# Two transformer blocks on one core: input tiles first in the queue, and ScalarE's copies spread over the steps of the first attention

## The chip, the cores and the metric

The kernel runs on one core of a Trainium2 chip. The metric is the device time of one execution in microseconds, and the time of a kernel is the median of its runs. Engines are named as usual: TensorE (PE) multiplies, VectorE (DVE) and ScalarE (ACT) do elementwise work, GpSimd (POOL) and SyncE (SP) here mostly issue transfers.

## The reference

One input `x` of 1 x 1024 x 1024 floats passes through two blocks. Only the beginning of the first one matters here:

```python
h = rms_norm(x, g_pre_mix)                 # mean of squares over the 1024 features
z = h @ w_in                               # 1024 x 2560
q, k, v, zu, zv = split(z)                 # 8 heads of 64
attn = dilated_attention(q, k, v, rel_bias)  # three windows (128,1), (512,4), (2048,16)
sgu = spatial_gating(gelu(zu), gelu(zv), ...)
mix = concat([attn, sgu]) @ w_out
x = x + rms_norm(mix, g_post_mix)
x = x + rms_norm(square(relu(rms_norm(x) @ w_ff1)) @ w_ff2, g_post_ffn)
```

The second block (modulated norms, a sparse attention that picks 256 keys by an index score, a convolution, another feed-forward layer) follows and isn't touched.

## The kernel before

Activations are held transposed, feature by token: `XT` is 128 partitions x 8 tiles x 1024 tokens. A weight matrix comes as slabs of 128 x 1024 (512 KB). Each product of a slab is made from three fp32r products: high part of the weights times high part of the input, high times low, low times high. ScalarE makes a slab's high part `whi` (L768), VectorE its low part `wlo` (L1715); an input tile is split in the same way into `XH` (L792) and `XL` (L1762). The order on every engine is written out by hand and tied together by semaphores.

**The prologue.** SP issues the transfers in this order: slab 0, `vec` (all vectors), `cst` (the constants: identity, ones, and others), the eight tiles of `XT`, slab 1. `vec` and `cst` count on `params_loaded`, the eight tiles on one semaphore, `x_loaded`. POOL loads `HOT` (a one-hot table) and `RB` (relative biases). TensorE waits for the constants and both tables, then multiplies `RB` by `HOT` (L1295, six products of 512 columns) into three PSUM tiles. VectorE copies them to `TAB` with the sign changed (L1792), from where POOL stores them to DRAM for later loads. VectorE next makes the low parts of slabs 0 and 1, and then adds up the squares of the tiles (L1722, L1725), which ScalarE makes (L778) into two buffers `SQ` after it has made the two high parts and all tiles are there. TensorE sums the total over partitions (L1257), VectorE and ScalarE turn this into the reciprocal root and a diagonal `DG` (L1749 to L1752, root on ScalarE L786), TensorE spreads it over all partitions (L1280). Then each tile is scaled (`HF`, L1770) and split, and the first two slabs are multiplied as the split tiles come (`product_pair`, L1237). Between its root and its splits ScalarE makes small copies that are needed much later (L805, L807) and a Silu (L809). After the splits ScalarE makes slab 2's high part, and evicts slab 0's product through a Gelu (L831); TensorE then turns it (L1312).

**The first attention.** It runs over 8 heads x 8 steps, `n = 8 h + d`. At each step TensorE makes scores by key (L1413), the values weighted by the probabilities of step `n - 3` (L1433, L1438, accumulated in `TP[1]` over a head's eight steps), and a guard product for step `n + 12` (L1386, of which VectorE takes the minimum, L1885). VectorE subtracts the bias strip (L1899), ScalarE takes Exp (L913). Between these, ScalarE has work per head:

```python
if d == 4 and h + 1 < HEADS:
    guard_row(h + 1)          # L881, the row of guard values, before that step's Exp
...                           # Exp of step n
if n in (10, 26):
    round_pair(n // 16 + 2)   # L861, L862: KR and QR of the next pair of heads
if d == 1 and 1 <= h < HEADS - 1:
    operands(h + 1)           # L872, L873: KA and QA of the next head
if d == 2 and h:
    sums_copy(h - 1)          # L890: TP[1] to OL; the next head's values wait for it
if d == 3 and h:
    inverse(h - 1)            # L896, L899: Ln and Exp of the sums
```

POOL scales a finished head, loads its bias strips and copies the row into `QA`.

Of the kernel before, what the change touches and what calls it, by code (L numbers as in the profile page):

```python
# [25 lines left out]
D = 1024  # L26
KT_N = D // P
# [3 lines left out]
HEADS = 8  # L31
# [16 lines left out]
RMS_EPS = 1e-6  # L48
# [94 lines left out]
def build(nc, slabs, ada, xT, vecs, lnrow, sgu_wT, rel_bias, positions, consts, hot, outT, dbg=None):  # L143
# [5 lines left out]
    def sem(name):  # L149
        return ctx.enter_context(nc.semaphore(name))  # L150
# [160 lines left out]
    hi_ready, lo_ready = sem("hi_ready"), sem("lo_ready")  # L311
    slab_done = sem("slab_done")
    psum_free = [sem(f"psum_free{b}") for b in range(2)]
    params_loaded, x_loaded, sgu_loaded = sem("params_loaded"), sem("x_loaded"), sem("sgu_loaded")
    hot_loaded, tab_made, tab_stored = sem("hot_loaded"), sem("tab_made"), sem("tab_stored")
    tab_copied = sem("tab_copied")
    bias_loaded = [sem(f"bias_loaded{b}") for b in range(2)]
# [175 lines left out]
    @block.sync  # L493
    def _(sp):
        def load(g, b):
            sp.dma_start(raw[b][:, :], slabs[bass.ds(g, 1), :, :].rearrange("a p n -> p (a n)")
                         if not isinstance(g, int) else slabs[g, :, :]).then_inc(raw_loaded[b], 16)

        load(0, 0)
        sp.dma_start(vec[:, :], vecs).then_inc(params_loaded, 16)  # L500
        sp.dma_start(cst[:, :], consts).then_inc(params_loaded, 16)
        for k in range(KT_N):
            sp.dma_start(XT[:, k, :], xT_v[:, k, :]).then_inc(x_loaded, 16)
        load(1, 1)
        first_loop, last_loop = (IN2 + 16 - 2) // 2, (OUT2 + 3 - 1) // 2
        assert IN2 % 2 == 0 and OUT2 % 2 == 1

        def next_slab(g):

            sp.wait_ge(lo_ready, g - 1)  # L510
            load(g, g % 2)

        def load_pairs(first, end):

            with sp.Fori(first, end) as t:
                for j in range(2):
                    sp.wait_ge(lo_ready, t * 2 + (1 + j))
                    load(t * 2 + (2 + j), j)

        def to_phases(j):  # L520

            sp.wait_ge(glu_ready, j + 1)
            sp.wait_ge(pool_seq, 3)
            sp.wait_ge(roped, 10)
            if j > 1:
                sp.wait_ge(conv_out, OUT_OF_TILE * (j - 1))
            for q in range(PHASES):
                for g in range(PHASES):
                    sp.dma_start(XP[j % 2][CB * q:CB * (q + 1), g, :], CUQ[CB * g:CB * (g + 1), j, q, :]).then_inc(phases_ready, 16)

        def to_channels(j, g):

            sp.wait_ge(conv_evicted, PHASES * j + g + 1)
            if j == 0:
                sp.wait_ge(conv_used, PHASES)
                sp.wait_ge(wt_moved, 1)
            for at_p in range(PHASES):
                p = PHASES - 1 - at_p
                sp.dma_start(YC[CB * g:CB * (g + 1), j, p * S // PHASES:(p + 1) * S // PHASES],
                             XP[j % 2][CB * at_p:CB * (at_p + 1), g, 0:S // PHASES]).then_inc(conv_out, 16)  # L540

        load_pairs(0, first_loop)
        next_slab(IN2 + 16)
        to_phases(0)
        next_slab(IN2 + 17)
        next_slab(IN2 + 18)
        to_phases(1)
        next_slab(OUT2)
        next_slab(OUT2 + 1)
        for j in range(PE_TILES):  # L550
            for g in range(PHASES):
                to_channels(j, g)
            if j + 2 < PE_TILES:
                to_phases(j + 2)
        next_slab(OUT2 + 2)
        load_pairs(last_loop, (STREAM - 2) // 2)
        sp.wait_ge(out_stored, 16 * KT_N)
# [199 lines left out]
    def _(act):  # L757
# [35 lines left out]
                               bias=bias(k) if bias else 0.0).then_inc(x_hi, 1)  # L793


        act.wait_ge(params_loaded, 32)
        hi(0, 0, 0)
        hi(1, 1, 0)
        squares(XT, lambda k: (x_loaded, 16 * KT_N))
        norm_root()  # L800
        act.wait_ge(params_loaded, 32)

        for q in range(PHASES):
# [3 lines left out]
                act.activation(phase_b[of_q, 4 * g:4 * g + 4], vec[CB * g:CB * (g + 1), VCOL["conv_b"]:VCOL["conv_b"] + 4],  # L807
                               ACT.Copy).then_inc(eye_ready, 1)
        act.activation(silc[:, :], vec[:, VCOL["c"]:VCOL["c"] + 8], ACT.Silu).then_inc(silc_ready, 1)  # L809
        splits(KT_N, 0)  # L810

        def to_qk(dst, scale, off):
            def body(m, g, b, h):
# [48 lines left out]
            act.activation(QR[m % 2][:, :].rearrange("p (t c) -> p t c", c=P)[:, :, ::-1],  # L862
                           QT[:, m, :].rearrange("p (t c) -> p t c", c=P), ACT.Copy, scale=-1.0).then_inc(rounded, 1)

        def operands(h):

            own = halves(h)[0]
            if h < 2:
                act.wait_ge(turned, 16)
            else:  # L870
                act.wait_ge(st_ready, NT * (h - 1))
            act.activation(KA[h % 2][0:DH, ::-1], KT[own, h // 2, :], ACT.Copy).then_inc(operands_ready, 1)  # L872
            act.activation(QA[h % 2][0:DH, :].rearrange("p (c u) -> p c u", c=4), by_class(QT[own, h // 2, :]),  # L873
                           ACT.Copy).then_inc(operands_ready, 1)

# [25 lines left out]
        def dilated_attention():  # L901

            act.preload_act_table_set("natural_log_exp_and_others")
            operands(0)
            guard_row(0)
            operands(1)
            round_pair(1)
            for n in range(NT * HEADS):
                h, d = divmod(n, NT)
                if d == 4 and h + 1 < HEADS:  # L910
                    guard_row(h + 1)
                act.wait_ge(st_taken, n + 1)
                act.activation(PT[n % 4][:, :], PT[n % 4][:, :], ACT.Exp).then_inc(pt_ready, 1)  # L913
                if n in (10, 26):
                    round_pair(n // 16 + 2)
                if n == 40:
                    hi_next(OUT1, OUT1 % 2, OUT1 // 2)
                if d == 1 and 1 <= h < HEADS - 1:
                    operands(h + 1)
                if d == 2 and h:  # L920
                    sums_copy(h - 1)
                if d == 3 and h:
                    inverse(h - 1)
                if n in (52, 60):
                    attended(n // 8 - 6)
            sums_copy(HEADS - 1)
            inverse(HEADS - 1)
# [123 lines left out]
        n = 0  # L1051
# [152 lines left out]
    def _(pe):  # L1204
# [84 lines left out]
            fill(ahead, g)  # L1289


        pe.wait_ge(params_loaded, 32)
        pe.wait_ge(hot_loaded, 32)
        for c in range(N_TABLE // HALF):
            last = pe.matmul((G[0], G[1], TP[0])[c // 2][0:HEADS, c % 2, :], RB[0:33, :], HOT[0:33, c * HALF:(c + 1) * HALF],  # L1295
                             start=True, stop=True)
        last.then_inc(tab_made, 1)
        pe.wait_ge(tab_copied, 1)
        norm_stat(KT_N, SSQ)
        norm_spread(DG)  # L1300


# [392 lines left out]
    def _(dve):  # L1695
# [37 lines left out]
            seq(dve.tensor_scalar(aa[:, :], aa[:, :], -0.5, 1.5, ALU.mult, ALU.add))  # L1733
            seq(dve.tensor_tensor(rstd[:, :], y0[:, :], aa[:, :], ALU.mult))

        def norm(width, eps, tiles=KT_N, sq=SQ, ssq=SSQ, dg=DG, first=0, stat=TP[1], between=None, last_on_pe=False, summed=None):
            for k in range(first, tiles - 1 if last_on_pe else tiles):
                add_square(k, sq, ssq)
            if between:
# [7 lines left out]
            else:  # L1747
# [3 lines left out]
            reciprocal_root()  # L1751
            t_diag.inc(dve.tensor_tensor(dg[:, :, :], ident.unsqueeze(1).broadcast_to([P, NT, P]),  # L1752
                                         rstd[:, :].unsqueeze(2).broadcast_to([P, NT, P]), ALU.mult))
            t_spread.wait(dve, 1)

        def split_norm(scale, bias, base):
# [30 lines left out]
                behind(KT_N - 1)  # L1787


        dve.wait_ge(tab_made, 1)  # L1790
        for b, made in enumerate((Gf[0], Gf[1], TPf[0])):
            last = dve.tensor_scalar(TAB[0:HEADS, b * S:(b + 1) * S], made[0:HEADS, :], -1.0, None, ALU.mult)  # L1792
        last.then_inc(tab_copied, 1)
        lo(0, 0)
        lo(1, 1)
        norm(D, RMS_EPS)
        dve.wait_ge(tab_stored, 16)
        split_norm(lambda k: V("g_pre_mix", k), None, 0)

# [613 lines left out]
```

## Time and profile before

| | |
|---|---|
| median of 3 runs | 2792.48 us (2790.01 to 2794.37) |
| profiled execution, its time | 2793.15 us |
| its span | 2791.4 us |
| busy: TensorE, VectorE, ScalarE, GpSimd | 2641.2, 1351.2, 836.0, 251.5 us |
| chain that ended last, by engine | PE 81%, DVE 9%, ACT 5%, issue 4% |
| mean granted TensorE clock | 0.978 |

The busy time of TensorE holds its waits inside a pipelined stream, so 95% of the span is no measure of how near it is to its peak. The chain says what the end of the kernel hung on, step by step back to the start; work on other engines that isn't in the chain costs nothing.

### The profile page before, as it was taken

The page shows a single profiled execution, that of the slowest core. Times are in us where ns is not written, and L with a number is a line of the kernel's source. Part 1 is how long each engine was busy: PE and PEld are TensorE (multiplying, and loading weights), DVE is VectorE, ACT ScalarE, POOL GpSimd, SP SyncE. Part 2 cuts the span into 40 slices and gives each one's busy share as a digit, 9 for nine tenths or more (in the row PEclk, how much of TensorE's full clock was granted, in tenths as well). Part 3 has the DMA queues.
Part 4 walks back from the last instruction along what each step waited for, and adds up shares of the span by engine and source line. Part 5 has one row for each costly group of instructions (what it writes and reads, how often), then busy time and mean ns, then how long its engine had stood idle before and what let it go on. Part 6 is the DMA issues. An engine that isn't in the chain of part 4 may idle for free.

```text
span 2791.4 us, 28672 instructions
## 1 busy us (share of the span) xinstructions
PE 2641.2 (95%) x11363; PEld 2088.6 (75%) x11363; DVE 1351.2 (48%) x1585; ACT 836.0 (30%) x1083; POOL 251.5 (9%) x269
## 2 busy tenths in 40 slices
PE   5999999989999999999999988898999999999996
PEld 3887667867888888888765766665878888888884
DVE  5242666356334343345748878786453232232333
ACT  3211345333112021121325575435332021120221
POOL 0000222002111121121001000211000000000000
PEclk9999999999999999999899998999999999999997
DMA  3211110214222222231310111001111111111111
GB/s 111 89 46 50 42 55 32 68 60 151 91 80 87 76 90 83 76 105 61 136 41 5 46 39 39 4 8 50 67 38 53 46 46 53 45 53 45 46 53 68
DMA packets 50376, 169.68 MB, mean 61 GB/s; under 512 B 7544, under 2 KB 11128, under 8 KB 50232
## 3 DMA queue, kind: packets, MB, share of 16 engines
q1 hardware_dynamic: 32544, 104.27, 11.4%
q0 software_dynamic: 17728, 63.98, 6.7%
q8 instruction: 72, 1.18, 0.2%
q14 instruction: 32, 0.25, 0.0%
HBM read 152.05 MB, written 12.68 MB: 59 GB/s over the span
## 4 chain that ended last, share of the span: by engine, by line
PE 81%; DVE 9%; ACT 5%; issue 4%; DMA 0%; SPq 0%; DVEq 0%; POOL 0%; ACTq 0%; POOLq 0%
PE G L1219 61%; PE G L1237 4%; PE G L1413 2%; PE TP L1642 2%; ACT TK L1071 2%; PE G L1560 1%; PE TP L1433 1%; PE TP L1386 1%; PE TP L1257 1%; DVE JUNK L2245 1%; PE G L1576 1%; ACT T L1057 1%; PE TP L1280 1%; PE TP L1438 1%; DVE wlo L1715 1%
## 5 line engine op out<-in xcount | busy, mean ns | idle before, releaser
L1219 PE MATMUL G<-XH,whi 128*128 128x512 f32 x1712 | 539.2, 396 | 15.2 <-DVE wlo L1715 13.1
L1219 PE MATMUL G<-XL,whi 128*128 128x512 f32 x1712 | 529.9, 391 | 0.0
L1219 PE MATMUL G<-XH,wlo 128*128 128x512 f32 x1712 | 529.8, 391 | 0.0
L768 ACT ACTIVATE whi<-raw 128x1024 fp32r<-128x1024 f32 x184 | 193.8, 1053 | 732.6 <-PE G L1219 671.0
L1219 PEld LDWEIGHTS G<-XH,whi 128*128 128x128 f32 x1712 | 319.8, 189 | 86.5 <-DVE wlo L1715 15.2
L1219 PEld LDWEIGHTS G<-XL,whi 128*128 128x128 f32 x1712 | 322.7, 189 | 67.8
L1219 PEld LDWEIGHTS G<-XH,wlo 128*128 128x128 f32 x1712 | 322.7, 188 | 67.8
L1219 PE MATMUL G<-UH,whi 128*128 128x512 f32 x1024 | 316.9, 391 | 0.0
L1219 PE MATMUL G<-UL,whi 128*128 128x512 f32 x1024 | 315.6, 389 | 0.0
L1219 PE MATMUL G<-UH,wlo 128*128 128x512 f32 x1024 | 315.5, 389 | 0.0
L1715 DVE TENSOR_TENSOR wlo<-raw,whi 128x1024 fp32r<-128x1024 f32 x184 | 224.3, 1220 | 149.4 <-ACT whi L768 149.1
L1219 PEld LDWEIGHTS G<-UH,wlo 128*128 128x128 f32 x1024 | 192.3, 188 | 40.0
L1219 PEld LDWEIGHTS G<-UL,whi 128*128 128x128 f32 x1024 | 192.3, 188 | 40.0
L1219 PEld LDWEIGHTS G<-UH,whi 128*128 128x128 f32 x1024 | 191.1, 188 | 38.6
L2026 DVE SCALAR_TENSOR_TENSOR XT<-G,mod,XT 128x1024 f32<-128x1024 f32 x32 | 41.1, 1285 | 249.1 <-PE G L1219 249.1
L2012 DVE TENSOR_TENSOR USQ<-RELU 128x1024 f32<-128x1024 f32 x32 | 39.2, 1225 | 192.2 <-ACT RELU L999 192.1
L995 ACT ACTIVATE RELU<-RELU 128x1024 f32<-128x1024 f32 x32 | 34.0, 1062 | 243.1 <-DVE RELU L2006 224.0
L1071 ACT ACTIVATE TK<-SC,cand 128x512 f32<-128x512 f32 (+2 forms) x93 | 82.8, 892 | 67.2 <-DVE cand L2132 67.2
L2026 DVE SCALAR_TENSOR_TENSOR XT<-G,XT 128x1024 f32<-128x1024 f32 x24 | 29.4, 1225 | 151.3 <-PE G L1219 151.3
L1991 DVE TENSOR_REDUCE RED<-ADA 128x128 f32<-128x1024 f32 x48 | 95.0, 1979 | 0.0
L999 ACT ACTIVATE RELU<-G 128x1024 f32<-128x1024 f32 x32 | 32.9, 1028 | 205.0 <-PE G L1219 205.0
L1885 DVE CUSTOM_DVE_ANT_0 JUNK<-TP,BIAS 128x1024 bf16<-128x1024 f32 x54 | 66.2, 1226 | 50.5 <-PE TP L1386 50.5
(304 smaller groups left out, 3195.2 us busy)
## 6 DMA issues: line engine op xcount, KB each, us to landing
raw<-slabs SPq DMA_DIRECT2D x184, 512.0 KB, 3.4
ADA<-ada POOLq DMA_DIRECT2D x48, 512.0 KB, 3.8
x_spill<-XT POOLq DMA_DIRECT2D x2, 4096.0 KB, 12.9
BIAS<-tab_spill POOLq DMA_DIRECT2D x8, 960.0 KB, 4.9
XT<-xT SPq DMA_DIRECT2D x8, 512.0 KB, 10.0
XRE<-xT POOLq DMA_DIRECT2D x8, 512.0 KB, 3.9
XRE<-x_spill POOLq DMA_DIRECT2D x8, 512.0 KB, 3.7
XT<-x_spill POOLq DMA_DIRECT2D x1, 4096.0 KB, 13.8
```

The lines of the kernel that those rows point to most:

```text
L768: act.activation(whi[b][:, :, :].rearrange("p k n -> p (k n)"), raw[b][:, :], ACT.Copy).then_inc(hi_ready, 1)
L995: act.activation(RELU[:, :], RELU[:, :], ACT.Square).then_inc(usq_ready, 1)
L1071: t_counted.inc(act.activation((TK1, TK2)[t_counted.n % 2][:, 0:w], SC[:, score_at(TOPK_TILE + n):score_at(TOPK_TILE + n + 1)], ACT.Sign, ...
L1219: last = pe.matmul(G[b][:, half, :], w[b][:, k, :], x[:, k, half * HALF:(half + 1) * HALF], start=(at_k == 0 and n == 0), stop=(at_k == KT ...
L1237: last = pe.matmul(G[b][:, half, :], w[b][:, k, :], x[:, k, half * HALF:(half + 1) * HALF], start=(at_k == 0 and n == 0), stop=(at_k == KT ...
L1413: last = pe.matmul(G[n % 4 // 2][:, n % 2, j * 2 * P:(j + 1) * 2 * P], keys, queries, start=True, stop=True)
L1642: pe.matmul(TP[1][:, u % 2, :], VO2[r][:, c, :], PT2[n % 4][:, :], start=(c == 0), stop=(c == i)).then_inc(p2_used, 1)
L1715: dve.tensor_tensor(wlo[b][:, :, :].rearrange("p k n -> p (k n)"), raw[b][:, :], whi[b][:, :, :].bitcast(F32).rearrange("p k n -> p (k n)" ...
L1885: dve.tensor_tensor_reduce(out=JUNK1[:, :], in0=flat(guard_out(p)), in1=BIAS[h % 2][:, 896 - i * P:896 - i * P + S], scale=1.0, scalar=HIG ...
L1991: dve.tensor_reduce(RED[a % 2][:, :], ADA[a % 2][:, :, :].rearrange("p k n -> p n k"), AX.X, ALU.add).then_inc(ada_red, 1)
L2012: dve.tensor_tensor(USQ[:, :], RELU[:, :], RELU[:, :], ALU.mult).then_inc(usq_ready, 1)
L2026: ins = dve.scalar_tensor_tensor(out=XT[:, m - 8, :], in0=Gf[b], scalar=scale(m - 8), in1=XT[:, m - 8, :], op0=ALU.mult, op1=ALU.add)
```

## The change

In the prologue SP issues the eight tiles of `XT` first, each with a semaphore of its own, then the constants, slab 0, the vectors and slab 1. ScalarE squares each tile when it has landed, before the high parts of slabs 0 and 1, and makes its small copies and the Silu after the splits. VectorE adds the squares first, then copies the table, waits for constants and vectors, and makes the low parts of slabs 0 and 1 after the diagonal (the new argument `ahead` of `norm`). TensorE starts the table products without a wait for the constants, waits for constants and vectors after them, and sums the squares before it waits for the table copies.

In the first attention `operands` becomes `key_operand` (after step 0) and `query_operand` (after step 3); `inverse` moves from step 3 to step 4, and the rounding of the next pair from `n` = 10, 26 to 14, 30.

```diff
@@ SP
+        for k in range(KT_N):
+            sp.dma_start(XT[:, k, :], xT_v[:, k, :]).then_inc(tile_loaded[k], 16)
+        sp.dma_start(cst[:, :], consts).then_inc(params_loaded, 16)
         load(0, 0)
         sp.dma_start(vec[:, :], vecs).then_inc(params_loaded, 16)
-        sp.dma_start(cst[:, :], consts).then_inc(params_loaded, 16)
-        for k in range(KT_N):
-            sp.dma_start(XT[:, k, :], xT_v[:, k, :]).then_inc(x_loaded, 16)
         load(1, 1)
@@ ScalarE, prologue
-        act.wait_ge(params_loaded, 32)
+        squares(XT, lambda k: (tile_loaded[k], 16))
         hi(0, 0, 0)
         hi(1, 1, 0)
-        squares(XT, lambda k: (x_loaded, 16 * KT_N))
         norm_root()
+        splits(KT_N, 0)
         act.wait_ge(params_loaded, 32)
...
         act.activation(silc[:, :], vec[:, VCOL["c"]:VCOL["c"] + 8], ACT.Silu).then_inc(silc_ready, 1)
-        splits(KT_N, 0)
@@ ScalarE, first attention
-        def operands(h):
+        def key_operand(h):
...
             act.activation(KA[h % 2][0:DH, ::-1], KT[own, h // 2, :], ACT.Copy).then_inc(operands_ready, 1)
+
+        def query_operand(h):
+
+            own = halves(h)[0]
             act.activation(QA[h % 2][0:DH, :].rearrange("p (c u) -> p c u", c=4), by_class(QT[own, h // 2, :]),
                            ACT.Copy).then_inc(operands_ready, 1)
...
-                if n in (10, 26):
-                    round_pair(n // 16 + 2)
                 if n == 40:
                     hi_next(OUT1, OUT1 % 2, OUT1 // 2)
-                if d == 1 and 1 <= h < HEADS - 1:
-                    operands(h + 1)
+                if d == 0 and 1 <= h < HEADS - 1:
+                    key_operand(h + 1)
                 if d == 2 and h:
                     sums_copy(h - 1)
-                if d == 3 and h:
+                if d == 3 and 1 <= h < HEADS - 1:
+                    query_operand(h + 1)
+                if d == 4 and h:
                     inverse(h - 1)
+                if n in (14, 30):
+                    round_pair(n // 16 + 2)
@@ TensorE
-        pe.wait_ge(params_loaded, 32)
         pe.wait_ge(hot_loaded, 32)
...
         last.then_inc(tab_made, 1)
+        pe.wait_ge(params_loaded, 32)
+        norm_stat(KT_N, SSQ)
         pe.wait_ge(tab_copied, 1)
-        norm_stat(KT_N, SSQ)
         norm_spread(DG)
@@ VectorE
+            if ahead:
+                ahead()
             t_spread.wait(dve, 1)
...
+        for k in range(KT_N):
+            add_square(k)
         dve.wait_ge(tab_made, 1)
...
         last.then_inc(tab_copied, 1)
-        lo(0, 0)
-        lo(1, 1)
-        norm(D, RMS_EPS)
+        dve.wait_ge(params_loaded, 32)
+        norm(D, RMS_EPS, first=KT_N, ahead=lambda: (lo(0, 0), lo(1, 1)))
```

## Rows read from the trace of the kernel before

**Rows 1.** The chain of waits, 0 to 110 us: start, length in us, what.
```profile
1.78 8.12 DMA cst<-consts
...
20.39 3.47 DVE TAB L1792 x3
23.86 2.27 DVE wlo L1715 x2
...
36.19 3.56 PE TP L1257 x16
...
50.21 24.23 PE G L1237 x96
```

**Rows 2.** Timeline, 0 to 50 us: start, length, engine, line, what [idle before].
```profile
4.83 1.28 ACT L768 ACT_TABLE_LOAD   x1 [4.83 <-DMA raw<-slabs]
...
21.24 1.06 ACT L768 ACTIVATE whi<-raw 128x1024 fp32r<-128x1024 f32 x1 [10.26 <-DMA raw<-slabs]
...
26.84 9.20 DVE L1725 TENSOR_TENSOR SSQ<-SSQ,SQ 128x1024 f32<-128x1024 f32 x7
...
40.09 0.21 ACT L805 ACTIVATE eye<-cst 32x32 f32<-32x32 f32 x1
...
42.62 3.78 PE L1280 MATMUL TP<-DG,cst 128*128 128x512 f32 x4 [2.88 <-DVE DG L1752]
...
45.87 0.21 ACT L809 ACTIVATE silc<-vec 128x8 f32<-128x8 f32 x1
```

**Rows 3.** The source view of L503, the input tiles: durations, first and last issue.
```profile
L503 SPq DMA_DIRECT2D XT<-xT x8: 432/538/1035, 2.3 to 6.9; - x8
...
DMA to landing us min/median/max: 7.5/10.0/13.1
```

**Rows 4.** DMA issues, 0 to 60 us: KB each, us to landing.
```profile
tab_spill<-TAB POOLq DMA_DIRECT2D x1, 96.0 KB, 3.4
RB<-rel_bias POOLq DMA_DIRECT2D x1, 1.0 KB, 7.6
```

**Rows 5.** Timeline, 60 to 80 us, ScalarE and TensorE.
```profile
70.45 1.06 ACT L768 ACTIVATE whi<-raw 128x1024 fp32r<-128x1024 f32 x1 [5.73 <-PE G L1237]
71.53 1.28 ACT L831 ACT_TABLE_LOAD   x1
72.82 1.03 ACT L831 ACTIVATE TT<-G 128x1024 f32<-128x1024 f32 x1
...
74.28 1.03 PE L1312 MATMUL TP<-cst,TT 128*128 128x128 f32 x8
```

**Rows 6.** Windows, heads 1 and 2: length, busy PE, PEld, DVE, ACT, POOL, PEclk, DMA.
```profile
331.06:358.53 27.47, 24.90 (x103) 17.54 (x102) 16.47 (x24) 12.97 (x19) 3.28 (x6) 0.88 0.16 51
358.53:382.24 23.71, 22.69 (x104) 16.68 (x104) 16.49 (x24) 11.19 (x16) 6.75 (x8) 1.00 0.17 59
```

**Rows 7.** Timeline of the first attention, heads 1, 2 and 7.
```profile
352.46 2.05 PE L1433 MATMUL TP<-PT,VONE 128*128 128x256 f32 x4 [2.57 <-ACT OL L890]
...
375.07 1.08 DVE L1899 TENSOR_TENSOR PT<-G,STRIP 128x512 f32<-128x512 f32 x1
375.18 2.01 ACT L873 ACTIVATE QA<-QT 64x1024 f32<-64x1024 f32 x1
...
377.75 1.06 ACT L890 ACTIVATE OL<-TP 128x512 f32<-128x512 f32 x2
...
378.48 1.10 PE L1433 MATMUL TP<-PT,VONE 128*128 128x256 f32 x4 [0.93 <-ACT OL L890]
378.77 0.63 ACT L913 ACTIVATE PT<-PT 128x512 f32<-128x512 f32 x1
...
381.99 0.27 ACT L881 ACTIVATE ROW<-TP 8x128 f32<-8x128 f32 x1 [0.55 <-PE TP L1393]
...
493.50 1.10 PE L1433 MATMUL TP<-PT,VONE 128*128 128x256 f32 x4 [0.66 <-ACT OL L890]
```

**Rows 8.** The source view of L1433, 320 to 505 us: idle before it, times.
```profile
ACT OL L890: 9.3, 7
```

More of the change, by code:

```diff
@@ L313, in build @@
     psum_free = [sem(f"psum_free{b}") for b in range(2)]
-    params_loaded, x_loaded, sgu_loaded = sem("params_loaded"), sem("x_loaded"), sem("sgu_loaded")
+    params_loaded, sgu_loaded = sem("params_loaded"), sem("sgu_loaded")
+    tile_loaded = [sem(f"tile_loaded{k}") for k in range(KT_N)]
     hot_loaded, tab_made, tab_stored = sem("hot_loaded"), sem("tab_made"), sem("tab_stored")
@@ L903, in dilated_attention @@
             act.preload_act_table_set("natural_log_exp_and_others")
-            operands(0)
+            key_operand(0)
+            query_operand(0)
             guard_row(0)
-            operands(1)
+            key_operand(1)
+            query_operand(1)
             round_pair(1)
@@ L1734, in reciprocal_root, with norm @@
             seq(dve.tensor_tensor(rstd[:, :], y0[:, :], aa[:, :], ALU.mult))
-        def norm(width, eps, tiles=KT_N, sq=SQ, ssq=SSQ, dg=DG, first=0, stat=TP[1], between=None, last_on_pe=False, summed=None):
+        def norm(width, eps, tiles=KT_N, sq=SQ, ssq=SSQ, dg=DG, first=0, stat=TP[1], between=None, last_on_pe=False, summed=None, ahead=None):
             for k in range(first, tiles - 1 if last_on_pe else tiles):
```

## Prediction

> **What bounds the kernel.** I read the chain that ended last first, because the table of shares alone (TensorE busy 95% of the span) would say that only matmuls count. The chain agrees for the long middle of the kernel, but its first 50 us run through other engines [rows 1]: a load, table matmuls, table copies and low parts on VectorE, the sum of squares, a column sum, and then the first product at 50.21. Whatever is taken out of that prologue is taken out of the time, since nothing later waits for a clock of its own: slabs are loaded when low parts are done. Next I read the timeline and the windows of the first attention, where TensorE is the longest engine but has short holes. The reader should look there for who ends each hole. The source view of L1433 names ScalarE's copy L890 for 9.3 us in 7 holes [rows 8].
>
> **Prologue, before.** The matmuls on the table start at 9.9, when the constants land (1.78 + 8.12), and end at 20.4. VectorE then copies the table (3.47), makes two low parts (2.27) and only then adds squares, to 36.1 [rows 1]. The squares run late too: ScalarE waits for slab 1 until 21.24 [rows 2], behind the wait for all input tiles. The column sum takes 3.56 and the first product starts 14.0 after the sum's start (50.21 less 36.19) [rows 1].
>
> **Prologue, after.** The column sum (L1257) needs three things:
> (a) The table matmuls, on the same queue: 20.4 if they start as before. They now need only the hot table and RB. RB is a transfer of 1 KB behind the hot table and took 7.6 [rows 4], so it must have landed shortly before the constants did; I take no change. Bounds: it lands no earlier than raw slab 0 did, 4.83 [rows 2], which would end the table matmuls 5 earlier (of which item (c) leaves 0.6 as gain); above, I allow the 1.5 us between two tiles (next item).
> (b) The squares and additions. Tile 0 landed at 2.3 + 7.5 = 9.8 and tile 7 at 6.9 + 13.1 = 20.0 [rows 3], 1.46 apart. First in the queue, tile 0 lands where raw slab 0 did, 4.83 [rows 2], and tile 7 at 4.83 + 7 x 1.46 = 15.1. The other bound: 896 KB (a slab, the vectors, the constants) no longer stand ahead of tile 7, at 1.46 per 512 KB 2.6 us; that gives 17.4. After landing, one square (ScalarE, 1.06 as for its neighbours) and one addition: the seven took 9.20, so 1.31 each [rows 2]. The additions end between 17.5 and 19.8, under the 20.4 of the table matmuls either way. I take 17.5; a tile stream as late as 21.2 would give the rival below.
> (c) The vectors, whose semaphore TensorE now waits for here. Slab 1, last in the queue, landed at 21.24 [rows 2]; the bytes are the same, so I keep that end, and the vectors land one slab earlier, about 19.8.
> So the sum starts at 20.4 instead of 36.19: **15.8 us**. The table copies (3.47) start at 20.4 as well and lie beside the sum (3.56), both end at 23.9; the variance needs both. Two low parts (2.27) lie beside the spread matmuls (3.78 [rows 2]), which are in front of the next VectorE work; without this cover they would cost 2.3. ScalarE makes the high parts of slabs 0 and 1 until about 22.3 and then loads the table for the root (1.28, as the load at 71.53 [rows 5]): 23.6, just under 24.0. SP issues the same transfers in another order, and only slab 0 lands later, by about 14, to about 18.5, while its high part is first wanted by a low part at 27. POOL's queue is not changed; its table store still follows the table copies at 23.9, 3.4 to landing [rows 4], before VectorE asks for it at 30.6.
> ScalarE's small copies (identity blocks, biases, Silu) took from 40.09 to 46.08 [rows 2] beside the spread. They move behind the eighth split. Before, ScalarE was idle for 5.73 there until slab 0's product ended [rows 5]. 5.99 do not fit in 5.73, so slab 2's high part, the table load and the Gelu eviction are 0.3 late. The eviction had ended at 73.85 and TensorE took it up at 74.28 [rows 5], 0.4 later. Cost: 0 expected, 0.3 at worst.
> Here a rule of the Trainium skill speaks against the change: page "ScalarE: Activation LUTs", section "What ACT_TABLE_LOAD costs", puts a switch of sets at about 2.66 us, since a drain comes with the load. With the trace the sum stays at 2763; with the page it would be the 2766 of the third rival. The load at 71.53 was followed by its activation 1.29 later [rows 5], so the trace doesn't show the drain.
>
> **First attention, before.** A head is 8 steps. TensorE may overwrite the accumulator of the last head only after L890 has copied it out, and L890 sits behind the exponentials of step 2 and, before those, both operand copies of step 1. In head 2 the scores of step 2 were ready for Exp at 376.15 (375.07 + 1.08), but ScalarE was in the QA copy (2.01), so L890 began at 377.75 and TensorE at 378.48, 0.93 late [rows 7]. In heads 1 and 3 the KR and QR copies come on top (about 1.06 each, as every ScalarE tile of 1024 columns [rows 2]): 2.57 late, and then the clock is down: 0.88 granted in that window, 1.00 in the next (full speed is 2.4 GHz, the other level 1.2) [rows 6, 7]. The holes of heads 1 to 6 are 9.3 less the last head's 0.66: 8.6 [rows 7, 8]. The clock costs, per event: window 27.47 against 23.71 is 3.76, less the hole's excess 1.64, 2.1; or 12% of 27.47, 3.3. I take 2.6, twice: 5.2.
>
> **After.** Step 0 has the KA copy (1.06; with Exp 1.7, in a step of 23.71 / 8 = 3.0), step 1 nothing, step 2 L890, step 3 the QA copy, step 4 the inverse (2.1), step 6 the rounding pair (2.1). Exp of step 2 then runs at 376.15, L890 at 376.7, and TensorE may go on 0.73 after that (378.48 less 377.75), at 377.4; it is itself free at 378.48 - 0.93 = 377.55. So the hole closes with 0.1 to spare. Queued behind the QA copy are the ROW copy and Exp of step 4: Exp of step 3 ran at 378.77, so QA ends by 381.3, while ROW could start at 381.99 - 0.93 = 381.06 [rows 7]; TensorE needs ROW only after a 1.1 us group of value matmuls. Behind the inverse stands Exp of step 5, used three steps later. KR and QR are first used in step 20 or 36 and now made at 14 and 30. Gain **8.6 + 5.2 = 13.8 us**; lower bound with the smaller clock term 12.8, upper 15.2.
>
> **Sum.** 15.8 + 13.8 = 29.6. The profiled execution took 2793.15 (span 2791.4), so 2763.6; it stands 0.7 above the median of 2792.48, so the median becomes **2763**.
>
> **Rivals.**
> Late squares: the eight tiles share the queues with the hot table so badly that tile 7 lands at the end of the stream, 21.2. Then 21.2 + 1.06 + 1.31 = 23.6 is the start of the column sum, 3.2 later: 2766. For it: tiles took up to 13.1 to land. Against: they are first in their queue now.
> Attention keeps its holes: 0.1 to spare is thin, and the last head, which has no operand copies, still had one of the seven holes [rows 8]. If 0.9 stays in each of six heads and only the clock loss and the excess go, 5.5 are missing: 2768. Against: that head's steps are shorter, for want of guard matmuls.
> Switch of sets: if a load in the middle of ScalarE's work costs twice its 1.28, the root's ends at 24.9, 0.9 after the variance, and the Gelu eviction, behind Silu's load and its own, is 0.3 + 2.6 late against the 0.4 to spare: 0.9 + 2.5 = 3.4 is missing, 2766. Against: the activation at 72.82 begins with the end of the load at 71.53 [rows 5]. This is how the change would go by the Trainium skill's rule of that page and section.
> Other side, slower: ScalarE's ROW copy. If it came late enough to hold TensorE 2.57 in each of heads 1 to 6, each would lose that and the clock's 2.6, 5.2 x 6 = 31, over the gain of 29.6: 2794. It decides from about 3.4 us later than worked out (0.8 of it the cover by value matmuls), where I find 0.2.
> No effect: the prologue is moved but the first product still waits for something at 50. I see no such thing: the slabs are in by 21.2 and the table is stored by 23.9 + 3.4.
>
> **How the numbers follow.** Forecast 74% (own range 2760 to 2766), late squares 8%, attention holes 8%, switch of sets 5%, opposite side 1.5%, no effect 1.5%, and 2% for a gain beyond 2760 (the spread and the first matmuls at the higher clock: half of 3.78 for the one, an estimate, and as much for the other). 0.2% of this time, 5.6 us, is about what a measurement can tell from no change. Every case but two ends far below it. Range 2759 to 2769: it takes in the three small rivals, the clock term's ends (+1.0, -1.4) and RB's landing (+1.5).
>
> **What would show it.** In the new profile: table matmuls from about 9.9 to 20.4; column sum right behind them; the first product at 34.4; no hole before the turn L1312 at about 58.5; L1433 with one hole for L890 (the last head) rather than seven; no window of the attention under 1.00; last exponential of the attention 29 to 30 earlier than at 502. Wrong if: table matmuls begin after 11.5, VectorE's additions outlast them, or heads take more than 22.8.

## The result and the profile after

The changed kernel took 2772.03 us in the median of 4 executions (2768.82, 2769.16, 2774.9, 2775.36), the kernel before 2791.48 (4 executions, 2790.01 to 2794.37). The ratio is 0.9928 (95% interval 0.9914 to 0.9942): 0.7% faster, clear of noise, but 9 us above my 2763 and 3 above the upper end of my range.

The profiled execution is the one of 2768.82 us, with a span of 2767.1, 24.3 less than before. Its chain of waits, 0 to 110 us, has these pieces (start, length, what):

```profile
2.09 7.17 DMA RB<-rel_bias
...
16.30 3.41 PE TP L1302 x4
19.71 3.52 PE TP L1265 x16
...
26.25 3.77 PE TP L1288 x4
...
38.62 19.34 PE G L1245 x84
57.96 0.87 PE TP L1320 x8
```

The column sum now follows the table matmuls without a gap, at 19.7 where it stood at 36.2 [rows 1]; additions, table copies and low parts are gone from the chain. The timeline of the same stretch shows what the steps of the prediction are about, the last square, the additions, the second high part and the load for the root, the root, the two low parts and the first product:

```profile
10.85 7.87 DVE L1733 TENSOR_TENSOR SSQ<-SSQ,SQ 128x1024 f32<-128x1024 f32 x6 [2.54 <-ACT SQ L779]
...
16.17 1.06 ACT L779 ACTIVATE SQ<-XT 128x1024 f32<-128x1024 f32 x1 [0.22 <-DMA XT<-xT]
...
19.72 1.06 ACT L769 ACTIVATE whi<-raw 128x1024 fp32r<-128x1024 f32 x1 [0.52 <-DMA raw<-slabs]
...
20.79 1.28 ACT L787 ACT_TABLE_LOAD   x1
...
23.52 0.21 ACT L787 ACTIVATE root<-var 128x8 f32<-128x8 f32 x1 [1.45 <-DVE var L1757]
...
26.02 2.35 DVE L1723 TENSOR_TENSOR wlo<-raw,whi 128x1024 fp32r<-128x1024 f32 x2
...
33.81 1.16 PE L1245 MATMUL G<-XH,whi 128*128 128x512 f32 x2 [3.81 <-DVE XL L1772]
```

The additions end at 18.7, a microsecond before the table matmuls do. The first product starts at 33.81 in place of 50.21: 16.4 less.

In the first attention the source view of the value matmuls (L1441, which was L1433) names one hole for the copy of the accumulator where there were seven [rows 8], the one of the last head; and the windows of heads 1 to 3 (columns as in [rows 6]) are even and at full clock:

```profile
  ACT OL L894: 0.7, 1
```

```profile
321.22:343.66 22.44, 22.35 (x103) 16.56 (x103) 16.45 (x25) 8.71 (x13) 3.28 (x6) 1.00 0.19 62
343.66:366.08 22.42, 22.33 (x104) 16.54 (x103) 16.47 (x25) 13.06 (x18) 6.76 (x8) 1.00 0.17 62
366.08:388.54 22.46, 22.38 (x104) 16.57 (x103) 16.44 (x25) 11.22 (x16) 6.75 (x8) 1.00 0.17 63
```

From the first scores to the first product behind the attention (L1245, L1237 before) it takes 169.84, against 184.33 before: 14.5 less. So both halves of the change did a little more than forecast, 16.4 + 14.5 = 30.9. Of these 24.3 arrived. The rest is lost between them, in the stretch from the last turns of the values (L1358, L1350 before) to the first scores. There the kernel before took 32.08 and the changed one 39.01, with the same instructions. Windows of that stretch, the changed kernel and then the kernel before:

```profile
271.68:310.69 39.01, 37.96 (x135) 25.36 (x134) 24.06 (x32) 16.59 (x15) 11.86 (x15) 0.69 0.07 26
```

```profile
288.16:320.24 32.08, 30.48 (x135) 19.95 (x134) 23.77 (x32) 16.57 (x15) 11.87 (x15) 0.89 0.09 31
```

The counts (x135, x32, x15) are equal, and so is the busy time of ScalarE and GpSimd to 0.02 us; TensorE has 7.5 us more of busy time, and its clock was granted at 0.69 in place of 0.89. No engine waits for anything new. 30.9 - 6.9 + 0.3 (the rest of the kernel, 2286.57 against 2286.83) = 24.3, the whole difference of the spans.

### The profile page after: what moved, and what is told of

Read it like the earlier page. It is cut to its first block, busy times and chain, and to the rows that moved or that the text cites. A ratio compares the mean times of both kernels' runs of the same rounds, so it can differ in the third digit from the quotient of the medians.

```text
span 2767.1 us, 28672 instructions
## 1 busy us (share of the span) xinstructions
PE 2641.7 (95%) x11363; PEld 2092.1 (76%) x11363; DVE 1351.1 (49%) x1585; ACT 836.1 (30%) x1083; POOL 251.8 (9%) x269
## 4 chain that ended last, share of the span: by engine, by line
PE 83%; DVE 8%; ACT 4%; issue 4%; DMA 0%; SPq 0%; DVEq 0%; POOL 0%; ACTq 0%; POOLq 0%
PE G L1227 62%; PE G L1245 4%; PE G L1421 2%; PE TP L1650 2%; ACT TK L1079 1%; PE G L1568 1%; PE TP L1394 1%; PE TP L1441 1%; PE TP L1446 1%; DVE JUNK L2256 1%; PE TP L1265 1%; PE G L1584 1%; ACT T L1065 1%; PE TP L1288 1%; PE G L1255 1%
## 5 line engine op out<-in xcount | busy, mean ns | idle before, releaser
L1227 PE MATMUL G<-XH,whi 128*128 128x512 f32 x1712 | 540.3, 397 | 14.3 <-DVE wlo L1723 12.4
L1245 PE MATMUL G<-XH,whi 128*128 128x512 f32 x192 | 63.2, 411 | 26.1 <-DVE XL L2326 9.3
## 6 DMA issues: line engine op xcount, KB each, us to landing
XT<-x_spill POOLq DMA_DIRECT2D x1, 4096.0 KB, 13.8
```

Source lines behind the costliest of these rows:

```text
L1227: last = pe.matmul(G[b][:, half, :], w[b][:, k, :], x[:, k, half * HALF:(half + 1) * HALF], start=(at_k == 0 and n == 0), stop=(at_k == KT ...
L1245: last = pe.matmul(G[b][:, half, :], w[b][:, k, :], x[:, k, half * HALF:(half + 1) * HALF], start=(at_k == 0 and n == 0), stop=(at_k == KT ...
```

## Experiments

Two theories. **C**: the granted clock falls in that stretch in some executions and not in others, since TensorE's work is thin there; the change has no part in it. **S**: the new order makes the stretch longer by itself. "Stretch" below is always that from the last value turns to the first scores, and a "dip" is a time in it at the lower clock, 1.2 GHz. Some expectations count the stretch from about 5.9 us later: their 33.1 and 26.2 are the 39.0 and 32.1 of this text.

### e1, e5, e10, e13: the changed kernel again

No edit. What was expected:

> The changed kernel once more, unaltered. Its profile has the work between the last value turn (L1358) and the first scores (L1421) of the first attention in 33.1 us, where the kernel before took 26.2, with the granted clock at 0.50 from 280 to 300 us. Theory C (the clock falls there or not by chance of time, the instructions being the same): over the executions the time takes more than one value, steps of some 6 us apart (2769 and 2775 so far), and in this profile the stretch may take 26 or 33. Theory S (the new order makes that stretch longer by itself): the stretch takes 33 again and every run the same time within 2 us.

> The changed kernel once more, on whatever chip this falls, beside the three below. Theory C (the time is a base plus what the clock takes in each execution): the runs lie between 2757 and 2775, ordered by their mean granted clock, some 2 us for each 0.001. Theory S: one value, 2759 or 2769.

> The changed kernel again, beside its version with full rows on one chip. So far 15 executions of it: nine between 2756.8 and 2762.2, six between 2768.7 and 2775.4. By that rate two of these lie above 2766.

> The changed kernel, fifth time: 21 executions so far, 15 of them under 2763 and six between 2768 and 2776. Theory C: again mostly 2757 to 2760, one or two higher, and a higher one has the lower granted clock.

| | executions, us | median | mean clock of each |
|---|---|---|---|
| first | 2768.8, 2769.2, 2774.9, 2775.4 | 2772.0 | 0.976, 0.976, 0.972, 0.972 |
| e1 | 2756.8, 2759.2, 2759.2, 2759.4, 2759.5, 2772.0 | 2759.3 | 0.981, 0.981, 0.981, 0.981, 0.981, 0.973 |
| e5 | 2757.2, 2757.5, 2759.7, 2762.2, 2768.7 | 2759.7 | 0.980, 0.981, 0.981, 0.980, 0.977 |
| e10 | 2757.4, 2757.4, 2757.4, 2757.7, 2759.2, 2759.5 | 2757.6 | 0.981, 0.980, 0.981, 0.981, 0.981, 0.979 |
| e13 | 2756.9, 2757.3, 2759.1, 2759.2, 2769.0, 2775.1 | 2759.2 | 0.981, 0.980, 0.981, 0.981, 0.976, 0.974 |

The time isn't one value, and the high ones are those with the lower clock. The kernel before spreads more: 66 executions between 2786.5 and 2809.0, median 2794.3. Over the 62 of them that were run beside the experiments, a straight line gives 2.2 us for each 0.001 of mean clock. Of e10's six I expected two above 2766; none was. The ratio in e1 is 0.9871 (0.9843 to 0.9900), in e13 0.9878 (0.9848 to 0.9908). The stretch took 32.1, 29.2, 29.3 and 32.1 in these four profiles. Windows of e10's:

```profile
271.25:300.55 29.30, 27.66 (x135) 18.59 (x134) 23.78 (x32) 16.57 (x15) 11.87 (x15) 1.00 0.09 34
```

Same kernel, same counts, 9.7 us less than in the first profile, at 1.00 in place of 0.69. Theory S falls. The timelines of the two show where they part. TensorE, first profile, then e10:

```profile
279.05 1.56 PE L1394 MATMUL G<-KR,QR 64*128 64x512 f32 x4 [0.61 <-DVE nega L1896]
280.54 1.97 PE L1375 MATMUL TP<-cst,NAT 128*128 128x128 f32 x8
282.44 2.07 PE L1394 MATMUL G<-KR,QR 64*128 64x512 f32 x4
```

```profile
278.63 1.16 PE L1394 MATMUL G<-KR,QR 64*128 64x512 f32 x4 [0.60 <-DVE nega L1896]
279.72 1.10 PE L1375 MATMUL TP<-cst,NAT 128*128 128x128 f32 x8
280.75 1.19 PE L1394 MATMUL G<-KR,QR 64*128 64x512 f32 x4
```

The hole before the guard products is the same to 0.01 us, and so is the work that led up to it (16 turns in 2.01, the guards in 2.1); within the next four products the one clock fell to 1.2 GHz and stayed there until about 303, the other stayed at 2.4.

There is a second place. In e1 the clock held behind that hole and fell behind the next one, 10 us later:

```profile
289.11 1.19 PE L1394 MATMUL G<-KR,QR 64*128 64x512 f32 x4 [0.57 <-DVE nega L1896]
290.25 1.72 PE L1260 MATMUL TP<-XH 128*128 128x512 f32 x4
```

So the 32.1 of e1, of e13 and of the kernel before is a dip too, a short one: without any the stretch takes 29.2 or 29.3.

### e2 and e3: one half of the change each

e2 is the changed kernel with the attention order of before:

```diff
+                if n in (10, 26):
+                    round_pair(n // 16 + 2)
                 if n == 40:
                     hi_next(OUT1, OUT1 % 2, OUT1 // 2)
-                if d == 0 and 1 <= h < HEADS - 1:
+                if d == 1 and 1 <= h < HEADS - 1:
                     key_operand(h + 1)
+                    query_operand(h + 1)
                 if d == 2 and h:
                     sums_copy(h - 1)
-                if d == 3 and 1 <= h < HEADS - 1:
-                    query_operand(h + 1)
-                if d == 4 and h:
+                if d == 3 and h:
                     inverse(h - 1)
-                if n in (14, 30):
-                    round_pair(n // 16 + 2)
```

e3 is the kernel before with the reverse of this edit.

> The prologue of the changed kernel with the attention order of before. Prologue by itself: 16.4 us by the first product's start (50.2 to 33.8). If the stretch before the attention runs at half clock here too (theory C in its form 'where it falls in time decides', the stretch being at the same time as in the changed kernel; and theory S in the form that the prologue's order does it): 16.4 - 6.9 = 9.5 less than before, about 2782, and its window 280 to 300 shows 0.50. If the attention's new order were the cause: 2775 and a window at 1.00.

> The attention order of the changed kernel with the prologue of before. By the chain the attention from first scores to last values took 184.4 before and 169.9 after, 14.5 less. Theory C: the stretch before the attention stands at the same time as in the kernel before, so it keeps its 26 us and the gain is 14.5: 2777. If the new order costs the 6.9 in that stretch (theory S, since its first copies are on ScalarE there): 2784 and a half-speed window at 296 to 316 us.

e2: median 2777.1 (12 executions, 2771.4 to 2792.5), ratio 0.9932 (0.9911 to 0.9953). e3: 2776.2 (12 executions, 2772.8 to 2791.1), ratio 0.9941 (0.9919 to 0.9962). Their medians come to 21.5 and 22.4 below the 2798.6 of the kernel before beside them. The two gains add up to more than the 39.3 between the medians of the kernel before and e1 on that chip; each median holds what the clock took in its own executions. In e2's profile the first product is at 33.6, as in the changed kernel, and the stretch took 29.3. In e3's, where the prologue is that of before, it took 38.9 at 0.69:

```profile
286.64:325.57 38.93, 37.89 (x134) 25.36 (x133) 24.02 (x32) 16.58 (x15) 11.86 (x15) 0.69 0.08 26
```

So the dip comes with the old prologue too, some 15 us later in time, and it stays away in e2's profiled execution, whose prologue is the new one: neither the prologue's order nor the place in time makes it by itself. My form of theory C that had it depend on the place in time alone was wrong for both runs.

e2 shows something else. Its attention has the seven holes of before, and took 187.4 in place of 184.3. One of them and the windows around it:

```profile
362.23 1.10 PE L1440 MATMUL TP<-PT,VONE 128*128 128x256 f32 x4 [0.94 <-ACT OL L894]
```

```profile
311.50:339.10 27.60, 25.03 (x104) 17.59 (x103) 16.70 (x25) 12.99 (x18) 3.28 (x6) 0.88 0.14 51
339.10:362.90 23.80, 22.86 (x93) 17.05 (x94) 14.78 (x22) 8.93 (x13) 6.75 (x8) 0.85 0.16 59
```

The clock was down in the first and in the second window, where the kernel before had 1.00 in its second [rows 6]: the hole of 2.6 cost the clock for longer in this execution. e3 and every profile of the changed kernel have 169.8 to 169.9 for the attention.

### e7: the operand copies back at step 1

The changed kernel with both operand copies at step 1; the rounding pair stays at steps 14 and 30, and the inverse at step 4:

```diff
-                if d == 0 and 1 <= h < HEADS - 1:
+                if d == 1 and 1 <= h < HEADS - 1:
                     key_operand(h + 1)
+                    query_operand(h + 1)
                 if d == 2 and h:
                     sums_copy(h - 1)
-                if d == 3 and 1 <= h < HEADS - 1:
-                    query_operand(h + 1)
```

> The changed kernel, but both operand copies at step 1 and so in front of the copy L890 of step 2, as before; the rounding pair stays at steps 14 and 30. If the operand copies make the holes of 0.9 in each of heads 1 to 6 (0.9 x 6 = 5.5) and the rounding pair made the rest: six holes of 0.7 to 1.0 for L890 in the profile, none of 2.6, no clock loss in the heads, 5.5 more than the changed kernel: about 2765. If holes of that size too cost the clock: windows under 1.00 within the heads and 2770 or more. If the holes are gone even so: 2759.

Median 2765.8 (6 executions, 2763.7 to 2779.1), beside 2759.7 for the changed kernel (e5, same chip). The attention took 175.5, 5.7 more than 169.8. The holes in heads 1 to 3:

```profile
340.62 1.10 PE L1440 MATMUL TP<-PT,VONE 128*128 128x256 f32 x4 [0.68 <-ACT OL L894]
...
364.13 1.10 PE L1440 MATMUL TP<-PT,VONE 128*128 128x256 f32 x4 [0.96 <-ACT OL L894]
...
387.38 1.10 PE L1440 MATMUL TP<-PT,VONE 128*128 128x256 f32 x4 [0.68 <-ACT OL L894]
```

Holes of 0.7 to 1.0, none of 2.6, and no loss of clock (1.00 over the whole attention), as expected. The six holes come to 4.9 (5.6 in seven, less the last head's 0.7), and the copies in front of L894 cost 5.7 in all. The other 8.8 of the 14.5 came with the moves that e7 keeps, rounding pair and inverse together; the inverse was not tried alone. The profiled execution itself had the dip in the stretch (39.0) and took 2775.7.

### e12: the old order of transfers

```diff
-        for k in range(KT_N):
-            sp.dma_start(XT[:, k, :], xT_v[:, k, :]).then_inc(tile_loaded[k], 16)
-        sp.dma_start(cst[:, :], consts).then_inc(params_loaded, 16)
         load(0, 0)
         sp.dma_start(vec[:, :], vecs).then_inc(params_loaded, 16)
+        sp.dma_start(cst[:, :], consts).then_inc(params_loaded, 16)
+        for k in range(KT_N):
+            sp.dma_start(XT[:, k, :], xT_v[:, k, :]).then_inc(tile_loaded[k], 16)
         load(1, 1)
```

> The changed kernel, but SP issues slab 0, vectors, constants, tiles, slab 1 as before; all else as changed. Prologue by its steps: tile 7 then lands at about 20, its square ends at 21.1, the additions at 22.4, and the column sum starts there in place of 19.4: 3.0 later, first product at 36.5 in place of 33.5, time 3 above the changed kernel's, 2762. If the tile order were the whole prologue gain: first product near 50. If it gave nothing: 33.5.

Timeline of its profile, the last square and the column sum:

```profile
18.75 1.06 ACT L779 ACTIVATE SQ<-XT 128x1024 f32<-128x1024 f32 x1 [0.27 <-DMA XT<-xT]
...
21.47 3.54 PE L1265 MATMUL TP<-cst,SSQ 128*128 128x1 f32 x16 [2.40 <-DVE SSQ L1733]
```

The column sum waits 2.40 for the additions and starts at 21.5, in e10 on the same chip at 19.2; the first products are at 35.6 and 33.3. So of the prologue's 16.4 the order of the transfers is worth 2.3 (I expected 3.0) and the order of the work on VectorE, ScalarE and TensorE the rest, 14.1, by subtraction. Median 2764.7 (2759.8 to 2778.5) beside 2757.6; its stretch took 44.6 in the profile, the longest of all: the dip that began behind the hole of 0.60 lasted until the first scores.

### e4, e6, e11, e14, e9: all rows in the first of each guard pair

The first eight guard products are made twice, for TensorE's sake alone. Here the first of each pair reads all 128 rows of the same tiles; its result is overwritten.

```diff
-            for _ in range(2 if p < NT else 1):
+            for rows in ((slice(0, P), own) if p < NT else (own,)):
                 for half in range(2):
-                    last = pe.matmul(guard_out(p)[:, half, :], QR[h // 2 % 2][own, i * P:(i + 1) * P],
-                                     KR[h // 2 % 2][own, half * HALF:(half + 1) * HALF], start=True, stop=True)
+                    last = pe.matmul(guard_out(p)[:, half, :], QR[h // 2 % 2][rows, i * P:(i + 1) * P],
+                                     KR[h // 2 % 2][rows, half * HALF:(half + 1) * HALF], start=True, stop=True)
```

> The changed kernel; only the first of the two identical guard products of each of the first eight guards reads all 128 rows of the same tiles in place of 64 (its result is overwritten by the second, so output and number of columns are unchanged). Theory C with the addition that thin work in TensorE (64 rows, transposes, short holes) lets the clock fall in that stretch: with all rows it stays up more often, 26 us in place of 33, and the time is 6 to 7 lower than the changed kernel's: 2762. Theory S, or a clock that looks at holes alone: no change, 2769 to 2775.

> The changed kernel with the first of each pair of guard products on 128 rows, again (the pair before it on one chip: 2759.7 against 2759.3 by the median, but its profile had no window under 1.00 between 40 and 560 us, and the stretch before the first scores took 29.5 in place of 32.1). If full rows keep the clock up in that stretch: again no such window in the profile, 29.5 us, and no run above 2762; if it was chance: a dip there in the profile, or runs above 2766 as often as the changed kernel has them.

> The changed kernel with full rows in the first product of each guard pair again. So far 11 executions, all between 2757.1 and 2760.7. If full rows prevent the dip: again none above 2762, stretch 29.5 in the profile. If it was the chip and chance: as many above 2766 as the changed kernel has beside it.

> Full rows in the first product of each early guard pair, fourth time: 17 executions so far between 2755.1 and 2760.7. If full rows prevent the dip, none above 2762 again, and the stretch from the last value turns to the first scores at 29.5 or 29.6 as in all four of its profiles. One above 2766 refutes it.

22 executions between 2755.1 and 2760.7, median 2759.7, mean 2759.1; the changed kernel's 27 have the median 2759.2 and the mean 2762.4, and eight of them lie between 2768.7 and 2775.4. The stretch took 29.54, 29.58, 29.61 and 29.55. By the median nothing is gained, where e4's text expected 6 to 7: in three of the four profiles the part behind the attention took 2286.9 to 2288.3, in e1's and e13's 2284.1 and 2284.3. Windows of e4's:

```profile
271.85:301.39 29.54, 28.37 (x134) 17.74 (x133) 23.75 (x32) 16.57 (x15) 11.88 (x15) 1.00 0.09 34
```

If the eight had fallen on the 49 executions by chance, none of them would lie among these 22 in 1 of 200 cases. Without the first four, which had no such kernel run beside them, it is 4 of 23 against 0 of 22, 1 in 17: likely, not settled.

The edit changes more than the rows. The hole before the third guard, where the long dips begin, was 0.60 or 0.61 wherever each guard was made twice on 64 rows; with full rows the first four products last longer (2.70 in place of 2.1 us) and the hole is 0.20, in all five profiles. e4's:

```profile
276.31 2.70 PE L1394 MATMUL G<-KR,QR 128*128 128x512 f32 x8
279.21 1.36 PE L1394 MATMUL G<-KR,QR 128*128 128x512 f32 x4 [0.20 <-DVE nega L1896]
```

So rows and hole were changed together, and no run here tells which of them keeps the clock. For the rows speaks that the next hole hardly changed (0.54 for 0.57) and the short dips behind it are gone as well: none in five profiles, where four of the seven 64-row profiles that came past the first hole without a dip have one. That is too few to settle it.

e9 is the same edit in the kernel before.

> The kernel before, with only the first of each of its eight pairs of guard products on all 128 rows. If full rows keep the clock up before the first scores: that stretch takes 29.5 in place of 32.1 or 39 in the profile, and no such dip; the rest of the runs keeps its spread (the holes of 2.6 in heads 1 and 3 still cost the clock), so 2786 to 2802 and a median some 3 to 7 under the kernel before. If it was chance: the same spread and median as before.

12 executions between 2788.7 and 2795.4, median 2790.8, against 2786.5 to 2807.0, median 2793.8; ratio 0.9990 (0.9975 to 1.0005). None of the twelve is above 2796, where six of the 17 beside them are, but the medians can't be told apart. The stretch took 29.6 at 1.00:

```profile
287.92:317.53 29.61, 28.43 (x135) 17.77 (x133) 23.80 (x32) 16.57 (x15) 11.88 (x15) 1.00 0.10 34
```

### e8: each early guard once

```diff
-            for _ in range(2 if p < NT else 1):
+            for _ in range(1):
```

> The changed kernel without the repeated product in each of the first eight guards (the repeat has no effect on the output; it is there for TensorE alone). It takes 8 x 0.66 us of work out of the stretch before the first scores. Theory C with activity: less work, so the clock falls there in every run and the stretch takes as long or longer, 32 to 39 us; time 2766 to 2775. If the clock were a matter of chance alone: the stretch gets shorter, 27 to 30, time 2755 to 2759.

6 executions between 2764.6 and 2769.0, at 0.974 to 0.977, median 2766.6: 6.9 above the changed kernel beside it, with less work. The window of the stretch:

```profile
271.25:307.48 36.23, 33.93 (x119) 21.59 (x118) 23.93 (x32) 16.53 (x15) 11.87 (x15) 0.67 0.08 28
```

16 products fewer, and 0.67. All six have a low mean clock, where of the five executions in e5, on the same chip, one has (0.977); the dip itself was seen in the one that was profiled. So the repeats are worth their time. But here too the hole changed with the work, to 1.42 from 0.60:

```profile
278.52 0.70 PE L1394 MATMUL G<-KR,QR 64*128 64x512 f32 x2 [1.42 <-DVE nega L1896]
```

The clock fell some 3 us behind it. Less work and a longer hole are two explanations, and this run doesn't part them; e8 and the full rows fit both.

### e15: the same, 2.5 us later

Before the diagonal, VectorE builds it twice more:

```diff
             if ahead:
+                for _ in range(2):
+                    seq(dve.tensor_tensor(dg[:, :, :], ident.unsqueeze(1).broadcast_to([P, NT, P]),
+                                          rstd[:, :].unsqueeze(2).broadcast_to([P, NT, P]), ALU.mult))
```

> The changed kernel with the diagonal built twice more on VectorE, 2 x 1.24 us in the chain, so that everything behind it comes 2.5 later in time, with the same instructions. By the chain alone: 2.5 above the changed kernel, 2760 to 2762. If the position in time of the stretch decides whether the clock falls there, and it is fixed to the start of the execution: all its executions move together, either to 2769 and more or to 2760. If each execution has its own position: a mixture as in the changed kernel, some at 2760 and some at 2770.

2759.7, 2760.0, 2760.3, 2762.0, 2777.1, 2777.3. A mixture, as in the changed kernel (e13, same chip: four to 2759.2, two from 2769.0): a shift by 2.5 us doesn't move all executions to one side. What differs from one execution to the next was not found.

## Why the prediction was wrong

**The step that failed** is in its first paragraph: "Whatever is taken out of that prologue is taken out of the time, since nothing later waits for a clock of its own". Between prologue and attention lies a stretch that I read no rows of and carried over at its 32 us, of which 2.8 were already a dip. How long its clock is down is drawn anew in each execution, and of all parts its length differs most: 29.2 to 39.0 for the changed kernel. In the profiled execution it took back 6.9 of the 30.9. In two of the first four executions another 6 were lost, at a mean clock of 0.972; these were not profiled, so where is open (e12 shows that the stretch can take 5.6 more than 39.0). Why all four of the first were high, when 19 of 23 later ones stayed under 2763, was not settled either: chip or chance.

Nor is the stretch the only part whose clock differs. Behind the attention, where no instruction was changed, the profiles of all runs took 2284.1 to 2288.3. Two windows of 20 us, both beginning 820 us behind the attention's end, the kernel before and then e1:

```profile
1324.57:1344.57 20.00, 20.00 (x93) 16.99 (x93) 11.66 (x18) 4.45 (x5) 2.16 (x4) 0.84 0.43 158
```

```profile
1293.42:1313.42 20.00, 19.55 (x102) 16.13 (x101) 11.66 (x18) 4.45 (x5) 2.16 (x4) 1.00 0.37 134
```

None of the three signs that I had named as "wrong if" came. The sign that failed is the last exponential of the attention: forecast 29 to 30 earlier, it came 24.0 earlier (477.96 against 502.01).

By its other steps the prediction held. **Table matmuls**: I took no change in their start; they started at 9.3 with RB's landing, 0.6 earlier, and slab 1 was there at 19.7, not 21.2. Landings differ between executions: with the old order of transfers both slabs were there by 20.7 in e12, and the first product, at 50.2 in the kernel before, was at 48.8 in e3 and at 49.9 in e9, where e1 and e10 on the same chips had 33.5 and 33.3. That makes the prologue worth 15.3 to 16.6. **Squares and additions**: tile 7 was there at 16.2, between my 15.1 and 17.4; the additions ended at 18.7, hidden. The even spacing by which I got there was not so (last section); the bounds were wide enough. **Vectors**: in time, the column sum did not wait. Forecast for the sum's start 20.4, measured 19.7; first product 34.4, measured 33.8. **Table copies, low parts**: beside the column sum and the spread, as said. **Small copies and Silu**: on ScalarE from 48.24 to 54.23, the high part of slab 2 right behind them, and the first turn followed the product pair without a gap: cost 0. e12 gives the order of the transfers 2.3 of the gain; the rival of late squares put 3.2 on it.

**Attention**: 13.8 forecast, 14.5 measured in that pair of profiles. Six holes gone, the last head's left, heads 1 to 3 of 22.4 to 22.5. TensorE's idle time there fell by 8.5 (10.7 to 2.2) for my 8.6, its busy time by 6.0 (173.6 to 167.6) for my 5.2 of the clock. e7 has the operand copies at 5.7 where I had 5.5. The clock's share was the least certain term (2.1 to 3.3 for an event), and two runs show that the rows of one execution don't bound it: the same two holes left the attention 3 longer in e2 than in the kernel before, and 1 shorter in e9.

**Rivals**. Late squares, holes that stay, the late ROW copy and no effect didn't come. The switch of sets didn't cost a drain: the load for the root ended at 22.07, the root at 23.52 waited for the variance, and the load at 52.73 was followed by Silu at 54.02, 1.29 later, in these rows of ScalarE's timeline:

```profile
52.73 1.28 ACT L810 ACT_TABLE_LOAD   x1
54.02 0.21 ACT L810 ACTIVATE silc<-vec 128x8 f32<-128x8 f32 x1
```

So the rule of the Trainium skill, page "ScalarE: Activation LUTs", section "What ACT_TABLE_LOAD costs", is not borne out in its drain here; its 1.28 for the load is what the trace has.

**The size of the error.** Over its 27 executions the changed kernel has a median of 2759.2, and the kernel before 2794.3 over 66, so the change is worth 35 (34 to 39 on each of the four chips of e1, e5, e10 and e13), not the 19.5 of the first comparison nor my 29.6. Of the 15.6 between 35.1 and 19.5, 12.8 are that the changed kernel's first four were high and 2.9 that the four of the kernel before were low. I worked from one profiled execution of a kernel whose executions differ by 22. The rows gave the chain right and the price of the clock only as it fell in that one. The 4 beyond 30.9 are not accounted for. That the holes of 2.6 are gone, and with them some of the high executions of the kernel before, would fit the spreads (2786 to 2809 before, 2757 to 2775 after), but was not measured. Between the profiles of the kernel before and of e1, whose stretches are equal, 33.9 are gained: 16.7 before the first product, 14.5 in the attention and 2.7 behind it, where the clock alone differs.

**The best version** is the changed kernel with full rows in the first guard of each pair: the same median, 2759.7, and no execution above 2760.7.

## What to carry to other kernels

Before summing up what a change takes away, look in the trace for stretches behind it in which the granted clock is under full speed, and run the kernel before several times: if its time follows its mean clock, one profile gives one draw, and the range must be as wide as those draws. Where an accumulator in PSUM is handed over, the copy that frees it should have nothing long in front of it on its engine in that step; a hole of 2.6 us cost 2.4 to 4.5 us more through the clock (what the attention of before, of e2 and of e9 took above 169.8, less their holes of 8.6, halved), one of 0.7 to 1.0 little more than itself (5.7 for six that sum to 4.9). Where TensorE waits between small products, a filler that uses all rows and shortens the wait is worth a try: it left the median as it was and no high execution, though by which of the two is open.

## What the runs showed of the hardware

Two executions of one program parted at the same instruction: with the same work and a hole of 0.6 us behind them, one clock fell to 1.2 GHz for some 24 us and the other stayed at 2.4 (39.0 against 29.3 us for the stretch). Taking eight guard repeats out of that stretch (hole 1.42) made the kernel slower by 6.9 us in the median, and reading 128 rows in place of 64 in them (hole 0.20) left no execution of 22 with the high time. With the old order of the queue the input tiles came in every 1.28 us, the last after 1.32 (e12's squares at 9.75 to 18.75), where I had 1.46 from the first and last landing. First in the queue, two came early and the third 3.8 us after the second, the others every 1.28 (squares at 4.36, 6.00, 9.76 and on to 16.17 in the changed kernel), so that going first brought the last tile forward by 3.1 (18.75 in e12, 15.69 in e10, one chip), between my 2.6 and 4.9.
